# Second feed-forward of a 2-layer network: block products of sums in three of its four groups

## The chip, the cores and the metric

One core of a Trainium2 chip runs the whole program. The metric is the device time of one execution in microseconds, the median of several.

## The reference

`x` has 512 tokens of 1024 features, all in f32. The network has a first part of two layers and a second part (two attention branches, a gated feed-forward with a convolution). The change lies in the feed-forward of layer 1 of the first part, with 4096 hidden features:

```python
for i in range(DEPTH):            # DEPTH = 2
    ...                           # a mixer (mLSTM in layer 0, spatial gating in layer 1)
    h = rmsnorm(x, norm_g[i, 2]) * (1.0 + sc2) + sh2
    y = jnp.square(jax.nn.relu(h @ ffn_w1[i])) @ ffn_w2[i]
    x = x + g2 * rmsnorm(y, norm_g[i, 3])
```

`ffn_w1[i]` is 1024 x 4096 and `ffn_w2[i]` is 4096 x 1024.

## The kernel before

Each f32 matrix product is made of three TensorE products: every operand is split into a high part in fp32r and a low part, the rest, in fp32r too, and hi·hi + hi·lo + lo·hi are added up in PSUM.

Weights come in tiles of 1 MB (1024 rows x 256 columns, in SBUF 128 x 2048). SyncE loads them into two buffers, `raw0` and `raw1` (`tile_in`: it waits until the tile that was in the buffer is split). ScalarE copies a tile to its high part (`split`, L1380), VectorE subtracts that from the tile to get the low part (`rest`, L1988). The parts go in turn to the homes W (`w_both_hi`, `w_both_lo`) and U (`u_both_hi`, `u_both_lo`), each with room for two tiles.

The feed-forward works in four groups of 1024 hidden features. The up part of a group has 4 tiles with 2 blocks of 128 hidden features each: a block is 8 x 3 matmuls, weights stationary, all 512 tokens moving, into PSUM bank 0 to 3 (`tile`, L615). ScalarE makes a block's relu, square and high part (`hidden`, L1651 to L1655), VectorE its low part (`g_rest`, L2398). The down part has 2 pairs of tiles: for each of four chunks of 128 tokens 8 x 3 matmuls, hidden features stationary, two tiles of weights (512 columns) moving (`tok_pair`, L687). VectorE adds each bank to `y_acc` in SBUF (`y_part`, L1995; in group 0 it copies, L1997). Groups 1 and 2 are a loop on each engine. PSUM bank reuse, tile reuse and hidden blocks are guarded by semaphores. The first tile pair of group 0 (`first_pair`, L789) and the last pair of group 3 (`last_pair`) run together with the norms of the phases around them (`boundary`).

GpSimd has no work in a feed-forward but for single columns of powers in the boundary. Elsewhere it multiplies or adds in SBUF: a bias of the spatial gating (L2787, 128x2048 in place), gated blocks (L2791, 128x512), splits of queries and keys (L2800 to L2812). The lines L1931, L2497, L2503 are VectorE's in those phases: weight low parts, low parts of gated blocks, an addition from PSUM. L651, L660, L1003 are TensorE's at the kernel's start. The conv phase near the end is written out in full, without a loop.

## Time and profile before

| | |
|---|---|
| median of 3 runs | 2071.27 us (2071.01 to 2071.88) |
| span of the profiled execution, first to last instruction | 2068.0 us |
| time of the profiled execution itself | not given; the median lies 3.3 us above the span |
| TensorE busy | 2035.2 us, 98% |
| VectorE busy | 1153.0 us, 56% |
| ScalarE busy | 859.5 us, 42% |
| GpSimd busy | 110.2 us, 5% |
| mean granted clock of TensorE | 0.997 |
| second feed-forward (its loop's groups) | 87.04 us each |

A row of a timeline gives start and duration in us, engine, line, operation, output, inputs and shapes, the count of instructions merged in the row (x), and in brackets how long the engine stood idle before it and what ended that.
### The profile page before, as it was taken

What the parts mean: (1) busy time and instruction counts of PE and PEld (TensorE: products, weight loads), DVE (VectorE), ACT (ScalarE), POOL (GpSimd) and SP (SyncE); (2) the same over time, 40 slices, a digit from 0 to 9 for tenths busy, and PEclk for the clock granted to TensorE, in tenths of its full rate; (3) what the DMA queues carried; (4) which work ended last, traced back from release to release, by engine and by line L of the source; (5) the groups of instructions that cost most, each with busy time, mean ns of one, the idle gap of its engine ahead of it and who ended that gap; (6) DMA issues with size and microseconds to landing.
All of it is one profiled execution on the core that took longest, in us unless ns stands there. A gap on an engine that the chain in (4) does not pass through costs nothing.

```text
span 2068.0 us, 27825 instructions
## 1 busy us (share of the span) xinstructions
PE 2035.2 (98%) x10894; PEld 1699.1 (82%) x10894; DVE 1153.0 (56%) x1758; ACT 859.5 (42%) x1291; POOL 110.2 (5%) x100
## 2 busy tenths in 40 slices
PE   7999999999999999999999999999999999999998
PEld 5898888888887888988888888876777798888887
DVE  4667867566565345654233335436679746546455
ACT  3334472424246222356233246345455545324233
POOL 0000000000001025110000001000111000000000
PEclk9999999999999999999999999999999999999999
DMA  9572337576553423423332331511132132323321
GB/s 315 163 242 85 127 111 238 192 226 198 171 167 115 152 77 102 113 82 102 102 101 83 101 112 56 150 52 31 45 117 84 43 112 96 109 81 102 102 72 71
DMA packets 230377, 248.32 MB, mean 120 GB/s; under 512 B 10978, under 2 KB 223357, under 8 KB 229365
## 3 DMA queue, kind: packets, MB, share of 16 engines
q1 hardware_dynamic: 187968, 202.45, 30.8%
q10 hardware_dynamic: 42293, 44.27, 6.6%
q8 instruction: 79, 1.29, 0.3%
q14 instruction: 37, 0.30, 0.1%
HBM read 237.63 MB, written 8.42 MB: 119 GB/s over the span
## 4 chain that ended last, share of the span: by engine, by line
PE 94%; DVE 2%; ACT 1%; DMA 1%; issue 1%; DVEq 1%; SPq 0%; ACTq 0%; POOL 0%; POOLq 0%
PE bank L615 37%; PE bank L687 32%; PE bank L789 4%; PE bank L1254 4%; PE bank L718 2%; PE bank L859 2%; PE bank L1226 1%; PE bank L1003 1%; PE bank L1237 1%; PE bank L1201 1%; PE bank L1310 1%; PE bank L1295 1%; PE bank L1204 1%; PE bank L1124 1%; PE bank L754 1%; DMA ada_head<-in_ada_w 1%
## 5 line engine op out<-in xcount | busy, mean ns | idle before, releaser
L615 PE MATMUL bank<-h_hi,w_both_hi 128*128 128x512 f32 x528 | 206.6, 391 | 0.0
L615 PE MATMUL bank<-h_hi,w_both_lo 128*128 128x512 f32 x528 | 205.5, 389 | 0.0
L615 PE MATMUL bank<-h_lo,w_both_hi 128*128 128x512 f32 x528 | 205.5, 389 | 0.0
L1380 ACT ACTIVATE u_both_hi<-raw 128x2048 fp32r<-128x2048 f32 x62 | 117.1, 1906 | 174.3 <-PE bank L687 134.4
L1988 DVE TENSOR_TENSOR u_both_lo<-raw,u_both_hi 128x2048 fp32r<-128x2048 f32 x62 | 141.6, 2290 | 84.9 <-ACT u_both_hi L1380 84.9
L1988 DVE TENSOR_TENSOR w_both_lo<-raw,w_both_hi 128x2048 fp32r<-128x2048 f32 x62 | 142.0, 2290 | 74.6 <-ACT w_both_hi L1380 74.5
L615 PE MATMUL bank<-h_hi,u_both_hi 128*128 128x512 f32 x464 | 180.9, 390 | 0.0
L615 PE MATMUL bank<-h_lo,u_both_hi 128*128 128x512 f32 x464 | 180.6, 389 | 0.0
L615 PE MATMUL bank<-h_hi,u_both_lo 128*128 128x512 f32 x464 | 180.6, 389 | 0.0
L1380 ACT ACTIVATE w_both_hi<-raw 128x2048 fp32r<-128x2048 f32 x62 | 117.4, 1907 | 143.5 <-PE bank L687 91.8
L687 PE MATMUL bank<-u_both_hi,g_hi 128*128 128x512 f32 x408 | 160.1, 392 | 0.0
L687 PE MATMUL bank<-u_both_hi,g_lo 128*128 128x512 f32 x408 | 158.9, 390 | 0.0
L687 PE MATMUL bank<-u_both_lo,g_hi 128*128 128x512 f32 x408 | 158.8, 389 | 0.0
L687 PE MATMUL bank<-w_both_hi,g_hi 128*128 128x512 f32 x376 | 146.8, 390 | 0.0
L687 PE MATMUL bank<-w_both_hi,g_lo 128*128 128x512 f32 x376 | 146.3, 389 | 0.0
L687 PE MATMUL bank<-w_both_lo,g_hi 128*128 128x512 f32 x376 | 146.3, 389 | 0.0
L615 PEld LDWEIGHTS bank<-h_hi,w_both_hi 128*128 128x128 f32 x528 | 99.1, 188 | 21.7 <-issue 1.5
L615 PEld LDWEIGHTS bank<-h_hi,w_both_lo 128*128 128x128 f32 x528 | 99.1, 188 | 20.8
L615 PEld LDWEIGHTS bank<-h_lo,w_both_hi 128*128 128x128 f32 x528 | 99.1, 188 | 20.5 <-issue 0.2
L2398 DVE TENSOR_TENSOR g_lo<-tmp,g_hi 128x512 fp32r<-128x512 f32 x64 | 43.6, 689 | 108.2 <-ACT g_hi L1655 108.2
L615 PEld LDWEIGHTS bank<-h_hi,u_both_lo 128*128 128x128 f32 x464 | 87.1, 188 | 18.3
L615 PEld LDWEIGHTS bank<-h_hi,u_both_hi 128*128 128x128 f32 x464 | 87.1, 188 | 17.9
(455 smaller groups left out, 4495.9 us busy)
## 6 DMA issues: line engine op xcount, KB each, us to landing
raw<-in_ffn_w SPq DMA_DIRECT2D x64, 1024.0 KB, 5.2
ada_raw<-in_ada_w ACTq DMA_DIRECT2D x40, 1024.0 KB, 5.2
raw<-in_w_up SPq DMA_DIRECT2D x22, 1024.0 KB, 5.1
raw<-in_b_w_in SPq DMA_DIRECT2D x16, 1024.0 KB, 5.4
raw<-in_w_in SPq DMA_DIRECT2D x15, 1024.0 KB, 5.5
raw<-in_a_w_in SPq DMA_DIRECT2D x12, 1024.0 KB, 6.4
ada_head<-in_ada_w SPq DMA_DIRECT2D x8, 1024.0 KB, 12.3
raw<-in_b_w_out SPq DMA_DIRECT2D x8, 1024.0 KB, 6.3
```

The source lines that it names most:

```text
L615: mm = pe.matmul(o, x, y, start=(k == 0 and j == 0), stop=(k == kc - 1 and j == 2))
L687: mm = pe.matmul(bank[c][:].rearrange("p (s n) -> p s n", s=2), x, y, start=(k == 0 and j == 0), stop=(k == kc - 1 and j == 2))
L718: mm = pe.matmul(bank[c][:, s * 256:s * 256 + 256], x, y[:, k], start=(k == 0 and j == 0), stop=(k == KB - 1 and j == 2))
L754: mm = pe.transpose(bank[4 + p][:, at_:at_ + P], src[:, c, b * P:b * P + P], ident)
L789: mm = pe.matmul(bank[2 * s + b][:, hs], x, y, start=(k == 0 and j == 0), stop=(k == KB - 1 and j == 2))
L859: mm = pe.matmul(bank[6][:], x, y, start=(k == 0 and j == 0), stop=(k == KB - 1 and j == 2))
L1003: mm = pe.matmul(bank[m][:], x[:, k], y[:, k], start=(k == 0 and j == 0), stop=(k == KB - 1 and j == 2))
L1124: mm = pe.matmul(bank[4 + g % 4][:, c * P:c * P + P], v_all[:, c, g * P:g * P + P], w_sT[:, g, :], start=True, stop=True)
L1254: mm = pe.matmul(bank[7][:], x, y, start=(k == 0 and j == 0), stop=(k == KB - 1 and j == 2))
L1380: act.activation(slot(where, s)[0], raw[s][:], ACT.Copy).then_inc(sem("hi_done"), 1)
L1988: dve.tensor_tensor(lo, raw[s][:], f32(hi), ALU.subtract).then_inc(sem("split_done"), 1)
L2398: dve.tensor_tensor(g_lo[:, y], T[m][:], f32(g_hi[:, y]), ALU.subtract).then_inc(sem("ffn_g"), 1)
```

## The change

In groups 0, 1 and 2 of this feed-forward the down part is calculated with seven products of quarter-size blocks (Winograd's form of Strassen's scheme) in place of eight. The tokens are cut in halves, the hidden features of the group in halves, the output features in halves: with A the hidden activations (A11, A12, A21, A22) and B the weights (B11 to B22), the left factors are A11, S1, S2, S4, S3, A12, A22 in this order, where S1 = A21 - A22, S2 = S1 - A11, S4 = S2 + A12, S3 = A11 - A21; the right factors are B11, T1, T2, B22, T3, B21, T4 with T1 = B11 + B12, T2 = T1 + B22, T3 = B12 + B22, T4 = T2 + B21. Up to signs, the banks hold running sums of products and VectorE adds them to the four quarters of `y_acc`. Group 3 stays as it was, but is written out.

- TensorE: a product is 2 chunks of tokens x 4 x 3 matmuls of 512 columns, 7 of them per group. `start` is not set for products 2, 3, 4 and 6, which go on in their banks.
- GpSimd: makes T1, T2, T3 and T4 (128x2048, in place in the raw buffers) and S3 (128x1024).
- ScalarE: high parts of 11 weight tiles per group (4 up, 7 down), relu and square of the blocks (the whole f32 block is kept in `g_full`), high parts of the seven left factors.
- VectorE: low parts of the 11 weight tiles and of the left factors, S1 (in two halves), S2 and S4, and 14 additions (in group 0 partly copies).
- SyncE: 8 loads of 1 MB per group as before, into four raw buffers (`raw2` and `raw3` lie in the second halves of home U); the weights' split parts go round three slots (W0, W1, U0), the left factors' round three others.
- Semaphores with names used once are merged to make room (`x_back`, `x_again` into `x_in`; `ada_head` into `part_in`; `gates_mm`, `tok_mm`, `t5_mm` into `single_mm`); no order changes by it.

```diff
-PHASES = [... ("ffn1", 32, 2), ...
+PHASES = [... ("ffn1", 10, 2), ...
+FAST = 3
+FAST_RING = [("W", 0), ("W", 1), ("U", 0)]
+FAST_NAMES = ["u0", "u1", "u2", "u3", "B11", "B12", "B22", "B21"]
+FAST_RAW = [[0, 1, 0, 1, 2, 3, 0, 1], [0, 3, 1, 2, 0, 3, 1, 2], [1, 3, 2, 0, 1, 3, 2, 0]]
+FAST_FROM = ["B11", "B11", "B11", "B22", "B12", "B21", "B11"]
...
@@ TensorE @@
+            def fast_product(g, m):
+                which, n = fast_low(g, 4 + m)
+                pe.wait_ge(sem(which), n)
+                pe.wait_ge(sem("f_a_lo"), 8 * g + [1, 3, 4, 5, 6, 7, 8][m])
...
+                for c in range(2):
+                    if m < 2:
+                        pe.wait_ge(sem("f_g"), 8 * g + 4 + 2 * m + c + 1)
+                    else:
+                        pe.wait_ge(sem("f_added"), 14 * g + 2 * (m - 2) + c + 1)
+                    cs = slice(c * P, c * P + P)
+                    for k in range(4):
+                        for i, (x, y) in enumerate([(ah, wh), (ah, wl), (al, wh)]):
+                            mm = pe.matmul(bank[2 * (m % 2) + c][:], x[:, k, cs], y[:, k], ...)
+                    mm.then_inc(sem("f_product"), 1)
+            for g in range(FAST):
+                for j in range(0 if g else 2, 4):
+                    fast_up(g, j)
+                for m in range(7):
+                    fast_product(g, m)
@@ ScalarE @@
+            for g in range(FAST):
...
+                fast_hi(g, 4)
+                act.drain()
+                fast_a(g, 0, quarter(0, 0))
+                fast_hidden(g, 4)
+                fast_hidden(g, 5)
+                fast_hi(g, 5)
+                act.wait_ge(sem("f_s"), 4 * g + 1)
+                fast_a(g, 1, s_sum, slice(0, 2))
+                fast_hidden(g, 6)
+                fast_hidden(g, 7)
+                act.wait_ge(sem("f_s"), 4 * g + 2)
+                fast_a(g, 1, s_sum, slice(2, 4))
+                fast_hi(g, 6)
+                act.wait_ge(sem("f_s"), 4 * g + 3)
+                fast_a(g, 2, s_sum)
+                fast_hi(g, 7)
+                act.wait_ge(sem("f_s"), 4 * g + 4)
+                fast_a(g, 3, s_sum)
+                fast_hi(g, 8)
...
@@ VectorE @@
+            for g in range(FAST):
+                for i in (2, 3, 4):
+                    fast_lo(g, i)
+                fast_a_lo(g, 0, 1, quarter(0, 0))
+                fast_lo(g, 5)
+                fast_s1(g, slice(0, 2))
+                fast_a_lo(g, 1, 2, s_sum, slice(0, 2))
+                fast_s1(g, slice(2, 4))
+                fast_a_lo(g, 1, 3, s_sum, slice(2, 4))
+                dve.drain()
+                dve.tensor_tensor(s_sum[:], s_sum[:], quarter(0, 0), ALU.subtract).then_inc(sem("f_s"), 1)
+                fast_lo(g, 6)
+                fast_a_lo(g, 2, 4, s_sum)
+                for c in range(2):
+                    fast_add(g, 0, c, 0, 0, ALU.add)
+                dve.tensor_tensor(s_sum[:], s_sum[:], quarter(0, 1), ALU.add).then_inc(sem("f_s"), 1)
+                for c in range(2):
+                    fast_add(g, 1, c, 2, 1, ALU.add)
+                fast_lo(g, 7)
+                fast_a_lo(g, 3, 5, s_sum)
+                fast_lo(g, 8)
+                fast_a_lo(g, 4, 6, s3_sum)
+                for c in range(2):
+                    fast_add(g, 2, c, 0, 1, ALU.subtract)
+                fast_a_lo(g, 5, 7, quarter(0, 1))
...
+                fast_lo(g, 9)
+                fast_lo(g, 10)
+                fast_a_lo(g, 6, 8, quarter(1, 1))
...
@@ GpSimd @@
+            for g in range(FAST):
+                pool.wait_ge(sem(fast_low(g, 4)[0]), fast_low(g, 4)[1])
+                pool.wait_ge(sem(FAST_IN[g, "B12"][0]), FAST_IN[g, "B12"][1])
+                fast_sum(g, "B11", "B12")
+                pool.wait_ge(sem("f_g"), 8 * g + 4)
+                pool.wait_ge(sem("f_a_lo"), 8 * g)
+                pool.tensor_tensor(s3_sum[:], quarter(0, 0), quarter(1, 0), ALU.subtract).then_inc(sem("f_pool"), 1)
+                pool.wait_ge(sem(fast_low(g, 5)[0]), fast_low(g, 5)[1])
+                pool.wait_ge(sem(FAST_IN[g, "B22"][0]), FAST_IN[g, "B22"][1])
+                fast_sum(g, "B11", "B22")
+                fast_sum(g, "B12", "B22")
+                pool.wait_ge(sem(fast_low(g, 6)[0]), fast_low(g, 6)[1])
+                pool.wait_ge(sem(FAST_IN[g, "B21"][0]), FAST_IN[g, "B21"][1])
+                fast_sum(g, "B11", "B21")
```

`fast_hi(g, i)` makes the high part of weight tile i (0 to 3 up, 4 to 10 for products 0 to 6), once its load or sum is there and the work on the tile three before it has ended; `fast_lo` makes the low part; `fast_a` and `fast_a_lo` do the same for a left factor; `fast_s1` makes a half of S1; `fast_add` adds a bank to a quarter of `y_acc`. On SyncE, in groups 1 and 2, u0 waits for low part 7 and T3 of the group before, u1 for low part 8, u2 for low part 9 and T4, u3 for low part 10, and B11, B12, B22, B21 for low parts 0, 1, 2, 3 of their own group.

## Rows read from the trace of the kernel before

**Rows 1.** The page: busy time of each engine; the chain that ended last, by line.

```profile
PE 2035.2 (98%) x10894; PEld 1699.1 (82%) x10894; DVE 1153.0 (56%) x1758; ACT 859.5 (42%) x1291; POOL 110.2 (5%) x100
...
PE bank L615 37%; PE bank L687 32%; PE bank L789 4%; PE bank L1254 4%; PE bank L718 2%; PE bank L859 2%; PE bank L1226 1%; PE bank L1003 1%; PE bank L1237 1%; PE bank L1201 1%; PE bank L1310 1%; PE bank L1295 1%; PE bank L1204 1%; PE bank L1124 1%; PE bank L754 1%; DMA ada_head<-in_ada_w 1%
```

**Rows 2.** Chain in order of time (start us, us): loop groups, and conv.

```profile
1098.67 43.52 PE bank L615 x192
1142.19 43.52 PE bank L687 x192
...
1833.03 87.04 PE bank L615 x384
```

**Rows 3.** Busy us of PE, PEld, DVE, ACT, POOL; clock, DMA share, GB/s.

```profile
1011.63:1098.67 87.04, 87.04 (x386) 72.07 (x385) 29.11 (x24) 29.57 (x32) 0.00 (x0) 1.00 0.30 97
```

**Rows 4.** Timeline of VectorE in a group of the loop.

```profile
1153.11 0.69 DVE L1995 TENSOR_TENSOR y_acc<-y_acc,bank 128x512 f32<-128x512 f32 x1 [4.14 <-PE bank L687]
1153.72 2.29 DVE L1988 TENSOR_TENSOR u_both_lo<-raw,u_both_hi 128x2048 fp32r<-128x2048 f32 x1
```

**Rows 5.** Timeline of ScalarE in a group of the loop.

```profile
1111.51 1.90 ACT L1380 ACTIVATE u_both_hi<-raw 128x2048 fp32r<-128x2048 f32 x1
1115.03 0.60 ACT L1651 ACTIVATE tmp<-bank 128x512 f32<-128x512 f32 x1 [1.62 <-PE bank L615]
1115.71 0.63 ACT L1653 ACTIVATE tmp<-tmp 128x512 f32<-128x512 f32 x1
```

**Rows 6.** Groups by shape, 128x1024 (busy us, mean ns of one).

```profile
L2569 DVE TENSOR_TENSOR w_both_lo<-raw,w_both_hi 128x1024 fp32r<-128x1024 f32 x2 | 2.5, 1225 | 19.6 <-ACTq L1777 19.6
...
L1491 ACT ACTIVATE x_sq<-x_tok 128x1024 f32<-128x1024 f32 x4 | 4.2, 1054 | 1.9 <-DMA x_tok<-in_x 1.7
```

**Rows 7.** Groups by shape, GpSimd's addition in place.

```profile
L2787 POOL TENSOR_TENSOR v_all<-v_all,lnb_bc 128x2048 f32<-128x2048 f32 x4 | 18.5, 4614 | 38.8 <-DVE v_all L2482 38.8
```

**Rows 8.** Timelines of VectorE and GpSimd at three places.

```profile
829.90 1.18 DVE L2497 TENSOR_TENSOR h_lo<-u_T,h_hi 128x512 fp32r<-128x512 f32 x1
831.00 0.68 DVE L2503 TENSOR_TENSOR tmp<-bank,bs_bc 128x512 f32<-128x512 f32 x1
...
828.92 1.60 POOL L2791 TENSOR_TENSOR u_T<-u_T,tmp 128x512 f32<-128x512 f32 x1 [4.95 <-DVE tmp L2503]
830.48 1.75 POOL L2791 TENSOR_TENSOR u_T<-u_T,tmp 128x512 f32<-128x512 f32 x1
...
812.37 2.28 DVE L1931 TENSOR_TENSOR w_both_lo<-raw,w_both_hi 128x2048 fp32r<-128x2048 f32 x1
812.40 3.39 POOL L2791 TENSOR_TENSOR u_T<-u_T,tmp 128x512 f32<-128x512 f32 x1
...
1490.87 1.27 POOL L2802 TENSOR_TENSOR kb_swapped_lo<-kb_swapped,kb_swapped_hi 128x512 fp32r<-128x512 f32 x1
1491.05 3.23 DVE L1931 TENSOR_TENSOR w_both_lo<-raw,w_both_hi 128x2048 fp32r<-128x2048 f32 x1 [1.08 <-ACT w_both_hi L1354]
```

**Rows 9.** Timeline at a short wait of TensorE in first_pair.

```profile
933.29 0.69 DVE L2060 TENSOR_TENSOR h_lo<-h_full,h_hi 128x512 fp32r<-128x512 f32 x1 [5.06 <-ACT h_hi L1430]
934.04 0.38 PE L789 MATMUL bank<-h_hi,w_both_hi 128*128 128x256 f32 x1 [0.53 <-DVE h_lo L2060]
...
934.26 0.28 PE L789 MATMUL bank<-h_lo,w_both_hi 128*128 128x256 f32 x1
```

**Rows 10.** Window at the start (columns as rows 3); timeline of TensorE there.

```profile
27.00:30.00 3.00, 2.71 (x7) 2.16 (x8) 3.00 (x3) 0.02 (x1) 0.00 (x0) 0.50 1.10 348
...
27.29 0.76 PE L1003 MATMUL bank<-h_hi,w_both_hi 128*128 128x512 f32 x1 [3.05 <-DVE h_lo L1979]
...
31.69 0.63 PE L1003 MATMUL bank<-h_lo,w_both_hi 128*128 128x512 f32 x1
32.12 0.52 PE L1003 MATMUL bank<-h_hi,w_both_lo 128*128 128x512 f32 x1
```

**Rows 11.** DMA issues: KB each, median us to landing.

```profile
raw<-in_ffn_w SPq DMA_DIRECT2D x64, 1024.0 KB, 5.2
```

More of the change, by code:

```diff
@@ L83, with fast_raw, fast_low, fast_block @@
 HALF = S // 2
+FAST = 3
[3 more added lines that the diff above has]
+FAST_FROM = ["B11", "B11", "B11", "B22", "B12", "B21", "B11"]
+FAST_POOL = ["T1", "S3", "T2", "T3", "T4"]
+FAST_IN, loads = {}, [2] * 4
+for g, buffers in enumerate(FAST_RAW):
+    for name, r in zip(FAST_NAMES, buffers):
+        if (g, name) not in ((0, "u0"), (0, "u1")):
+            loads[r] += 1
+            FAST_IN[g, name] = (f"part_in{r}", 16 * loads[r])
+def fast_raw(g, name):
+    return FAST_RAW[g][FAST_NAMES.index(name)]
+def fast_low(g, i):
+    return "f_lo", 11 * g + i - 1
+def fast_block(g, b):
+    return 8 * g - 4 + b + 1
+def fast_pool(g, name):
+    return 5 * g + FAST_POOL.index(name) + 1
 ADA_HEAD = 8
@@ new lines, in _ @@
+            fast_split(FAST - 1, 9)
+            sp.wait_ge(sem("f_pool"), fast_pool(FAST - 1, "T4"))
+            tile_in(0, r3(0), cols(w1, FAST * 1024, 256), t0 + 2)
+            fast_split(FAST - 1, 10)
+            tile_in(1, r3(1), cols(w1, FAST * 1024 + 256, 256), t0 + 3)
+            for j in range(2, 4):
+                tile_in(j % 2, r3(j % 2), cols(w1, FAST * 1024 + j * 256, 256), t0 + 2 + j)
+            for j in range(4):
+                tile_in(j % 2, r3(j % 2), cols(w2[:, FAST, :], j * 256, 256), t0 + 6 + j)
@@ L591, in evacuated, with tile @@
                 pe.wait_ge(sem(f"evac{bk}"), q + 1)
-            def tile(t, s, q, hi, lo, kc=KB, tok=False, ready=None, after_block=None, parts=None, banks=None):
+            def tile(t, s, q, hi, lo, kc=KB, tok=False, ready=None, after_block=None, parts=None, banks=None, added=None):
                 pe.wait_ge(sem("split_done"), t + 1)
@@ L1133, in _, with fast_up @@
             last_pair("b_out", t0 + 6, q0 + 3, "U", g_hi, g_lo)
-            ffn("ffn1", "b_out", False)
+            t0, q0 = T0["ffn1"], N0["ffn1"] // 4
+            first_pair("b_out", t0, q0)
+            def fast_up(g, j):
+                which, n = fast_low(g, j)
+                pe.wait_ge(sem(which), n)
+                wh, wl = (w.rearrange("p (k n) -> p k n", k=KB) for w in fast_slot(11 * g + j))
+                for b in range(2):
+                    m, bs = 2 * (j % 2) + b, slice(b * P, b * P + P)
+                    if j < 2:
+                        pe.wait_ge(sem("f_added"), 14 * g - (1 - b if j == 0 else 3 - b))
+                    else:
+                        pe.wait_ge(sem("f_g"), 8 * g + m + 1)
+                    for k in range(KB):
+                        for i, (x, y) in enumerate([(wh, h_hi), (wh, h_lo), (wl, h_hi)]):
+                            mm = pe.matmul(bank[m][:], x[:, k, bs], y[:, k], start=(k == i == 0), stop=(k == KB - 1 and i == 2))
+                    mm.then_inc(sem("f_up"), 1)
@@ new lines, in _ @@
+            for g in range(FAST):
[3 more added lines that the diff above has]
+                    fast_product(g, m)
+            for j in range(4):
+                tile(t0 + 2 + j, j % 2, q0 + 1 + j // 2, h_hi, h_lo, parts=slot("WU"[j // 2], j % 2),
+                     added=14 * FAST - 1 if j == 0 else None)
+            tok_pair(t0 + 6, q0 + 3, "W", g_hi, g_lo, ready=(sem("ffn_g"), G0["ffn1"] + 4))
+            last_pair("ffn1", t0 + 8, q0 + 4, "U", g_hi, g_lo)
@@ new lines, in _ @@
+            for j in range(6):
+                s, q = j % 2, q0 + 1 + j // 2
+                rest(u0 + 1 + j // 2, s, "UW"[j // 2 % 2])
+                for b in range(2):
+                    if j < 4:
+                        m, y = 2 * s + b, 2 * j + b
+                        dve.wait_ge(sem("ffn_ghi"), GHI0["ffn1"] + y + 1)
+                        dve.tensor_tensor(g_lo[:, y], T[m][:], f32(g_hi[:, y]), ALU.subtract).then_inc(sem("ffn_g"), 1)
+                    else:
+                        y_part(q, 2 * s + b, 0, True)
@@ L2792, in _, with fast_sum @@
             boundary("b_out")
+            def fast_sum(g, to, more):
+                a, b = (f_raw[fast_raw(g, name)][:] for name in (to, more))
+                pool.tensor_tensor(a, a, b, ALU.add).then_inc(sem("f_pool"), 1)
+            for g in range(FAST):
+                pool.wait_ge(sem(fast_low(g, 4)[0]), fast_low(g, 4)[1])
[11 more added lines that the diff above has]
+                fast_sum(g, "B11", "B21")
             boundary("ffn1")
```

204 lines of the change are left out of this document (187 added, 17 removed).

## Prediction

> **What bounds the kernel now.** I read the page's first lines before anything else: TensorE works 98% of the span, VectorE 56%, ScalarE 42%, GpSimd 5%, and the chain that ended last is nearly all TensorE, 37% of the span at the line of the up products and 32% at that of the down products [rows 1]. Then the chain in order of time, inside the second feed-forward: 192 matmuls of 512 columns take 43.52 us, up and down alike, with no gap between them [rows 2]. That is 0.2267 us per matmul and 87.04 us per group. In such a group VectorE works 29.1 us and ScalarE 29.6, at the full granted clock [rows 3]. So a matmul taken away is worth 0.2267 us, as long as the other engines deliver in time. Their durations come next [rows 4, 5, 6, 7], then the rows where VectorE and GpSimd read SBUF together [rows 8], and last what TensorE's restart and clock do after a wait [rows 9, 10].
>
> **What is removed.** A fast group has the same 192 up matmuls, but its down part has 7 products of 24 matmuls in place of 192: 168, thus 24 fewer. The form stays (128x128 stationary, 512 columns moving), so the price stays: 24 x 0.2267 = 5.44 us a group, and 16.3 us for three. A fast group takes 81.60 us if nothing waits: products begin at 43.52, one every 5.44.
>
> **What is added, per group.** VectorE: 11 weight low parts at 2.29 [rows 4] = 25.2; the low parts of the sums of hidden blocks, six of 128x1024 and two of 128x512, 6 x 1.22 [rows 6] + 2 x 0.69 = 8.7; S1 in halves, S2 and S4: 2 x 0.69 + 2 x 1.22 = 3.8; 14 additions to y at 0.69 [rows 4] = 9.7. Together 47.4 us, where there were 29.1. The copies that group 0 has in place of additions have the same length. ScalarE: 11 weight high parts at 1.90, 8 hidden blocks at 0.60 + 0.63 [rows 5], the high parts of sums 6 x 1.05 [rows 6] + 2 x 0.63: 38.3 us. GpSimd: four weight sums of 128x2048 in place, the form of the one that takes 4.61 us in this trace [rows 7], and S3 at about 2.4: 20.8 us. Each engine has room in 81.6 us on average; the question is the second half of the group.
>
> There VectorE's order is strict. I laid it out, with time 0 at a group's first up matmul; consecutive VectorE instructions start 0.08 us before the one before has ended [rows 4], and a semaphore costs 0.04 to 0.06 us [rows 5, 9] (the block before the row at 1115.03 ends at 1098.67 + 72 x 0.2267 = 1114.99). **Without any contention:** hidden block 7 is done at 44.9 (its matmuls end at 43.52), S1's second half at 45.6, its high part on ScalarE 46.25, its low part 47.0, S2 48.2, low part 6 50.5, that of S2 51.6, two additions 52.8, S4 53.9, two additions (product 1 ends at 54.4) 55.7, low part 7 58.0, that of S4 59.1. Product 3 wants it at 59.84. So it is just in time, with 0.7 us to spare, and the gain would be all of 16.3 us.
>
> **GpSimd's sums get in the way.** The low parts and S sums read two SBUF tensors each on VectorE, as GpSimd's sums do. Where these meet in the trace, one stands until the other is over [rows 8]: the low part at 829.90 takes 1.18 us in place of 0.69, ending 0.56 after GpSimd's product has; the next GpSimd product ends 1.15 after that low part. With a longer one, GpSimd's product at 812.40 takes 3.39 in place of 1.27, ending 1.14 after a VectorE instruction of 2.28; and VectorE's weight low part at 1491.05 takes 3.23, ending 2.14 after the GpSimd instruction. They take turns: a VectorE instruction already waiting got in between two GpSimd ones that stood back to back. VectorE instructions with one PSUM operand are not held (0.68 at 831.00, beside GpSimd); the additions to y are of that kind. So a sum holds VectorE's SBUF instructions for 4.61 less 0.15 of its own start: 4.46 us.
>
> The Trainium skill (SBUF — State Buffer, section Who interferes with whom) states the same for any length: a VectorE instruction with two SBUF inputs and a GpSimd instruction that reads SBUF exclude each other for the whole instruction. By that rule the full 4.46 holds; the trace agrees for 0.6 to 2.3 us, and shows no case of 4.6.
>
> Now the same order with it. T1 runs in the up part, where VectorE has time; nothing waits. T2 may start once low part 5 is done at 38.14: S1's first half is already running, so T2 holds from 38.70 to 43.16. The first half of S1's low part, which waited, takes 43.16 to 43.72; T3 43.72 to 48.18. S1's second half has been ready since 44.9 and now ends at 48.74; ScalarE's copy 49.40, low part 50.11. **Product 1, due at 48.96, starts 1.2 us late.** S2 ends at 51.4, low part 6 at 53.6, that of S2 at 54.7, all before T4, which waits for low part 6, gets in: T4 holds 54.7 to 59.15. The additions of product 0 run beside it until 55.9, but S4 stands 3.3 us and ends at 60.2. Additions of product 1 61.4, low part 7 63.65, that of S4 64.8. Product 2 ended at 61.05: **product 3 starts another 3.8 us late.** After that there is slack again: product 4 (due 70.3) has its last input at 68.8, product 5 (75.7) at 74.1, product 6 (81.2) at 77.4, the next group (86.6) at 80.8. Each of the two restarts costs 0.06 us from semaphore to matmul and about 0.10 in the first one (0.38 where the next has 0.28) [rows 9]: 0.3 us.
>
> **Work moved that costs nothing.** Loads: eight of 1 MB per group as before, 5.2 us each [rows 11], into four buffers. The tightest is the first tile of the last group: issued after low part 9 at 74.1, it lands at 79.3, high part 81.2, low part 83.5, for a start at 86.6: 3 us of cover. The others have over 5. VectorE is then behind with two additions, which the last group covers. The wait for all 42 product halves ahead of the last group's ScalarE work ends where its U split could start before, as a buffer was only free then. Renamed semaphores add nothing. GpSimd's queue held nothing in this phase but the boundary's powers, which come after. Writing groups 1 and 2 out in place of a loop adds instructions; conv is written out and its chain has no gaps, 87.04 us for 384 matmuls [rows 2], so zero.
>
> **Sum.** -16.3 + 3 x (1.2 + 3.8 + 0.3) = -16.3 + 15.9 = -0.4 us on a span of 2068.0. The profile gives no time of its own for its execution; 3.3 us lie between its span and the median of 2071.27, and I keep these. **Forecast 2070.9 us.** Some 12 handovers a group with 0.05 us of doubt each, and 0.1 us on each of three sums, give 0.9 a group: 2068 to 2074 for this case.
>
> **Rivals.**
> *No mutual standing at this length* (GpSimd reads so slowly that both get by): then -16.3, 2055.0. For it: no row has a sum of 4.6 us beside such a VectorE instruction. Against it: [rows 8], in both directions. 0.09.
> *A long sum lets go in pieces*, say of the 1.15 us that one of 512 elements takes: S1's second half and S4 stand 1.2 in place of 3.3 us, so the stalls fall by some 4 to about 1 us a group: -13, 2058; with larger pieces anything up to the forecast. GpSimd's time grows in proportion (1.27 for 512, 4.61 for 2048), which fits one pass as well as four. 0.17.
> *The clock falls in product 3's wait.* TensorE would stand 3.8 us. At the start of the kernel it stood 3.05 us, after light work with another wait in it, and the granted clock was 0.50 from 27 to 30 us, the lower level of 1.2 GHz: matmuls of 512 columns came every 0.43 us until about 32.1 [rows 10]. Some 4.8 us at half pace lose 2.4 us; three times, +7.2: 2078. It decides for slower from two falls on. Against it: before these 3.8 us TensorE is dense, unlike there, and after the short wait before 934.04 no matmul is slow [rows 9]. 0.14, half of that with two or more falls. The Trainium skill (TensorE: Matmul & The Clock Gate, section Rules for kernel authors) advises against idle gaps of this order between bursts of matmuls; by that rule the fall comes and 2078 would hold.
> *GpSimd wins where I let VectorE go first*: T4 ahead of S2's low part makes product 2 late by 3.2 and product 3 by 1.5, 5.9 us of stall in place of 5.0: 2073.6. With T3 ahead as well, or a low part standing twice, 1.5 more a group, 2078. 0.12.
> *As forecast*: 0.48.
>
> **Numbers.** A measurement tells about 0.2%, 4.1 us. Faster by more: 0.09 + 0.15 of the pieces = 0.24. Slower by more: 0.08 of the clock, 0.05 of GpSimd's turns, 0.05 for a longer wait elsewhere in the same order = 0.18. Within: 0.58. The range for 8 in 10 runs from 2057 (all but the first rival and the smallest pieces) to 2078.
>
> **What the profile of after would show.** TensorE's group near 86.9 us instead of 81.6, with two gaps per group, at products 1 and 3, put down to VectorE's low parts of the hidden sums; low parts or S sums on VectorE of 4 to 5 us where 1.2 or 0.7 was due; GpSimd sums of 4.6 us, longer where a VectorE instruction stood first. If those VectorE instructions keep 0.69, 1.22 and 2.29 beside running sums, the first rival holds; waits of about 1 us mean pieces; a granted clock below 1.00 in products 3 and 4 means the third. I am wrong, too, if gaps stand at another product, or if loads release ScalarE's high parts.

## The result, and the profile after

The changed kernel takes 2077.23 us (median of 6, 2075.51 to 2078.69), the kernel before 2070.83 us beside it (2069.56 to 2071.88): a ratio of 1.0033, 95% interval 1.0021 to 1.0044. It is slower by 6.4 us; the forecast was 0.4 us faster. The profiled execution has a span of 2076.9 us and a time of 2078.69 us, 1.8 us more than its span.

The page, first its busy lines, which answer to [rows 1]:

```profile
PE 2027.3 (98%) x10822; PEld 1689.6 (81%) x10822; DVE 1231.7 (59%) x1797; ACT 882.9 (43%) x1300; POOL 180.5 (9%) x115
```

TensorE has 72 matmuls fewer, as it should, but is busy only 7.9 us less, not 16.3: the ones that are left have become slower somewhere. The chain in order of time shows where, in the second fast group; it answers to the two 43.52 us pieces of [rows 2]:

```profile
1014.06 43.53 PE bank L1251 x192
...
1058.95 3.87 DVE s_sum L2791
...
1070.05 4.35 DVE s_sum L2818
1074.39 1.20 DVE y_acc L2802 x2
1075.59 2.21 DVE w_both_lo L2780
1077.80 1.22 issue
1079.03 23.65 PE bank L1269 x96
1102.68 3.40 PE bank L1251 x15
```

A group lasts from 1014.06 to 1102.68, 88.62 us; before it was 87.04, predicted were 86.9. Two of VectorE's sums in SBUF are in the chain with 3.87 and 4.35 us; alone they take 0.69 and 1.22. (An instruction "stands" here when it has been issued and waits for the other engine; the timeline counts that in its duration.) Then 96 matmuls take 23.65 us. At 0.2267 us each they should take 21.76: this is a piece of pure TensorE work, with no wait in it, that is 1.89 us too long. The timelines of VectorE and GpSimd for that stretch, beside [rows 4, 8]:

```profile
1053.47 4.32 DVE L2786 TENSOR_TENSOR a_lo<-s_sum,a_hi 128x512 fp32r<-128x512 f32 x1 [0.70 <-ACT a_hi L1941]
1058.95 3.86 DVE L2791 TENSOR_TENSOR s_sum<-g_full 128x512 f32<-128x512 f32 x1 [1.16 <-ACT g_full L1934]
...
1067.63 1.22 DVE L2786 TENSOR_TENSOR a_lo<-s_sum,a_hi 128x1024 fp32r<-128x1024 f32 x1
1068.77 1.28 DVE L2802 TENSOR_TENSOR y_acc<-y_acc,bank 128x512 f32<-128x512 f32 x2
1069.96 4.43 DVE L2818 TENSOR_TENSOR s_sum<-s_sum,g_full 128x1024 f32<-128x1024 f32 x1
...
1077.72 1.21 DVE L2786 TENSOR_TENSOR a_lo<-s_sum,a_hi 128x1024 fp32r<-128x1024 f32 x1
```

```profile
1052.25 10.01 POOL L3134 TENSOR_TENSOR raw<-raw,raw 128x2048 f32<-128x2048 f32 x2 [3.00 <-DVE w_both_lo L2780]
1067.79 5.52 POOL L3134 TENSOR_TENSOR raw<-raw,raw 128x2048 f32<-128x2048 f32 x1 [5.54 <-DVE u_both_lo L2780]
```

These are T2 with T3, and T4. The first half of S1's low part ends at 1057.79, 43.73 after the group's start (predicted 43.72); S1's second half at 48.75 (48.74); S4 at 60.33 (60.2). T4 was issued 0.16 after S2's low part had begun and stood first (5.52 in place of 4.61); the two additions of product 0 ran beside it at 0.64 each. Now TensorE at the two waits, and the clock around product 3 (windows of the three us before it and the six behind, columns as in [rows 3]):

```profile
1064.30 0.47 PE L1269 MATMUL bank<-w_both_hi,a_hi 128*128 128x512 f32 x1 [1.28 <-issue]
...
1079.03 0.47 PE L1269 MATMUL bank<-w_both_hi,a_hi 128*128 128x512 f32 x1 [3.57 <-issue]
...
1080.86 0.63 PE L1269 MATMUL bank<-w_both_hi,a_hi 128*128 128x512 f32 x1
1081.29 0.63 PE L1269 MATMUL bank<-w_both_lo,a_hi 128*128 128x512 f32 x1
```

```profile
1076.00:1079.00 3.00, 0.00 (x0) 0.00 (x1) 3.00 (x3) 3.00 (x3) 0.00 (x0) 1.00 0.03 11
1079.00:1082.00 3.00, 2.97 (x9) 2.44 (x10) 3.00 (x2) 1.98 (x2) 0.00 (x0) 0.67 0.93 272
1082.00:1085.00 3.00, 3.00 (x11) 2.35 (x11) 2.91 (x5) 0.00 (x0) 0.00 (x0) 0.76 1.03 334
```

Product 1 is 1.3 us late, and product 3 starts at 64.97 of the group (predicted 64.9). The view puts both waits down to "issue", but product 3 starts 0.10 us after S4's low part has ended (1077.72 + 1.21 = 1078.93), its last input by the order above. From 1 us behind product 3's wait the matmuls come every 0.43 us, as in [rows 10], and the granted clock drops below 1.00: 1.2 GHz for a while, then 2.4 again. The same happens in all three groups: 23.64, 23.65 and 23.68 us for the 96 matmuls, after waits of 3.57, 3.57 and 3.60 us.

Where the 8.9 us between the two spans lie, by landmarks of the two chains: 0.8 before the first fast group (946.33, then 947.14), 4.8 in the three groups (239.38, then 244.19), none from there to the 192 matmuls that open the attention (151.63 and 151.65), **3.2 in the attention** (314.33, then 317.55), none after (416.33, 416.37). The attention isn't touched by the change. The 0.8 is within what traces differ by there: the same place comes at 945.38 us in short_sums and at 948.69 us in memsets, two kernels described below that differ in nothing up to it. The medians are 6.4 us apart and not 8.9; the traced execution is the slowest of its six.

### The profile page after: what moved, and what is told of

Read it like the earlier page. It is cut to its first block, busy times and chain, and to the rows that moved or that the text cites. A ratio compares the mean times of both kernels' runs of the same rounds, so it can differ in the third digit from the quotient of the medians.

```text
span 2076.9 us, 27540 instructions
## 1 busy us (share of the span) xinstructions
PE 2027.3 (98%) x10822; PEld 1689.6 (81%) x10822; DVE 1231.7 (59%) x1797; ACT 882.9 (43%) x1300; POOL 180.5 (9%) x115
## 4 chain that ended last, share of the span: by engine, by line
PE 88%; DVE 6%; ACT 2%; DMA 2%; issue 1%; DVEq 1%; ACTq 0%; SPq 0%; POOL 0%; POOLq 0%
PE bank L716 31%; PE bank L788 25%; PE bank L1251 5%; PE bank L1401 4%; PE bank L890 4%; PE bank L1269 3%; PE bank L960 2%; PE bank L1373 1%; PE bank L1104 1%; PE bank L1384 1%; PE bank L819 1%; PE bank L1348 1%; PE bank L1457 1%; PE bank L1442 1%; PE bank L1351 1%
## 5 line engine op out<-in xcount | busy, mean ns | idle before, releaser
L2240 DVE TENSOR_TENSOR w_both_lo<-raw,w_both_hi 128x2048 fp32r<-128x2048 f32 x52 | 119.1, 2290 | 69.0 <-ACT w_both_hi L1527 65.9
L716 PE MATMUL bank<-h_hi,u_both_hi 128*128 128x512 f32 x368 | 143.5, 390 | 0.0
L716 PE MATMUL bank<-h_hi,u_both_lo 128*128 128x512 f32 x368 | 143.2, 389 | 0.0
L716 PE MATMUL bank<-h_lo,u_both_hi 128*128 128x512 f32 x368 | 143.2, 389 | 0.0
L788 PE MATMUL bank<-u_both_hi,g_hi 128*128 128x512 f32 x312 | 122.7, 393 | 0.0
L788 PE MATMUL bank<-u_both_hi,g_lo 128*128 128x512 f32 x312 | 121.6, 390 | 0.0
L788 PE MATMUL bank<-u_both_lo,g_hi 128*128 128x512 f32 x312 | 121.4, 389 | 0.0
L788 PE MATMUL bank<-w_both_hi,g_hi 128*128 128x512 f32 x280 | 109.4, 391 | 0.0
L788 PE MATMUL bank<-w_both_lo,g_hi 128*128 128x512 f32 x280 | 108.9, 389 | 0.0
L2194 DVE SCALAR_TENSOR_TENSOR ada_acc<-ada_raw,c_act,ada_acc 128x256 f32<-128x256 f32 x182 | 88.2, 484 | 14.1 <-issue 0.6
L2183 DVE TENSOR_TENSOR w_both_lo<-raw,w_both_hi 128x2048 fp32r<-128x2048 f32 x29 | 67.3, 2320 | 39.9 <-ACT w_both_hi L1501 39.5
```

Source lines behind the costliest of these rows:

```text
L716: mm = pe.matmul(o, x, y, start=(k == 0 and j == 0), stop=(k == kc - 1 and j == 2))
L788: mm = pe.matmul(bank[c][:].rearrange("p (s n) -> p s n", s=2), x, y, start=(k == 0 and j == 0), stop=(k == kc - 1 and j == 2))
L2183: dve.tensor_tensor(w_lo[s][:], raw[s][:], f32(w_hi[s][:]), ALU.subtract).then_inc(sem("split_done"), 1)
L2194: i = dve.scalar_tensor_tensor(o, src[:, k], c_act[:, k:k + 1], o, ALU.mult, ALU.add)
L2240: dve.tensor_tensor(lo, raw[s][:], f32(hi), ALU.subtract).then_inc(sem("split_done"), 1)
```

## Experiments

Times are medians; ratios are to the kernel before on the same chip. "Group" is the second fast group in the chain.

**The sums' cost as a whole.** short_sums leaves out nearly all of the four weight sums, so GpSimd has next to nothing left that could hold VectorE:

```diff
-                pool.tensor_tensor(a, a, b, ALU.add).then_inc(sem("f_pool"), 1)
+                pool.tensor_tensor(a[:, 0:64], a[:, 0:64], b[:, 0:64], ALU.add).then_inc(sem("f_pool"), 1)
```

> The four weight sums on GpSimd work on 64 of 2048 columns (the rest of each sum is left out); everything else as in the changed kernel. Theory (GpSimd's sums hold VectorE's instructions with two SBUF inputs, that makes both waits per group, and the long wait lowers the clock): no wait at products 1 and 3, clock 1.00, group 81.6 us in place of 88.6, 3 x 7.0 = 21 less than the changed kernel: 2056. Rival (VectorE's own 47 us of work and the handovers bound the second half, the sums only add to it): waits of over 1 us per group stay, 2062 to 2070.

2055.91 us, ratio 0.9918 (0.9903 to 0.9934); group 81.60. The kernel gives wrong numbers, as its sums are left out. So the matmul price, the rest of the order and the loads were sized rightly, and all 16.3 us come back once the sums hold nobody.

**The clock by itself.** busy_wait fills product 3's wait with 12 matmuls that nobody reads:

```diff
+                if m == 3:
+                    for _ in range(12):
+                        pe.matmul(bank[5][:], h_hi[:, 0, 0:P], h_hi[:, 0], start=True, stop=True)
```

> Ahead of product 3 TensorE gets 12 matmuls of 512 columns into bank 5, which nobody reads: 2.7 us of the 3.6 us that it waits there. Theory (the clock falls because TensorE stands 3.6 us): the wait's end stays where it was, the clock stays at 1.00 in products 3 to 6, the group is 1.9 us shorter: 3 x 1.9 = 5.6 less than the changed kernel, 2071.6. Rival (the slow matmuls after the wait come from the weight loads that land at the same time, or from anything else than the standing): they stay slow, 2077, or more by what the extra matmuls delay.

2073.28 us, ratio 1.0006 (0.9997 to 1.0015): some 4 us below the changed kernel's median (5.6 by the two ratios), by *more* work. The chain:

```profile
1073.49 2.72 PE bank L1258 x12
1077.07 22.03 PE bank L1272 x96
1099.10 0.91 PE bank L1251 x4
```

The 96 matmuls take 22.03 in place of 23.65, and the windows behind the wait show 1.00 (22.00 to 22.04 in the three groups). The group takes 87.00: the 86.9 of the prediction. So the clock costs 1.6 us a group here, some 4.9 in all, and the wait alone what was predicted.

**Who holds whom.** memsets puts three memsets of the same buffer in place of each sum (the sums are left out), of 5.7 us together:

```diff
-                pool.tensor_tensor(a, a, b, ALU.add).then_inc(sem("f_pool"), 1)
+                pool.memset(a, 0.0)      # three times, a drain between
```

> Each of the four weight sums is replaced by three memsets of the same 128x2048 buffer (some 5.5 us of GpSimd time, longer than a sum, writing to SBUF and reading nothing from it; the sums are left out). Theory (what VectorE's two-input instructions stand for is GpSimd's reading): VectorE keeps 0.69, 1.22 and 2.29, no waits, group 81.6, 2056 as with the short sums. Rival (any GpSimd instruction on SBUF, or a late start of GpSimd's semaphores, holds them): waits at products 1 and 3 as in the changed kernel or longer, 2077 or more.

2059.43 us, ratio 0.9945 (0.9929 to 0.996); group 81.60, as in short_sums. The time is 3.5 us above that of short_sums all the same; in the two traces 3.3 us lie ahead of the first fast group (948.69 and 945.38 us). GpSimd, then VectorE:

```profile
1052.34 1.82 POOL L3134 MEMSET raw<- 128x2048 f32 x1
1054.28 1.81 POOL L3136 MEMSET raw<- 128x2048 f32 x1
1056.21 1.81 POOL L3138 MEMSET raw<- 128x2048 f32 x1
```

```profile
1054.84 0.69 DVE L2786 TENSOR_TENSOR a_lo<-s_sum,a_hi 128x512 fp32r<-128x512 f32 x1 [0.70 <-ACT a_hi L1941]
1055.62 1.22 DVE L2813 TENSOR_TENSOR s_sum<-s_sum,g_full 128x1024 f32<-128x1024 f32 x1
1056.77 2.28 DVE L2780 TENSOR_TENSOR u_both_lo<-raw,u_both_hi 128x2048 fp32r<-128x2048 f32 x1
```

VectorE keeps its 0.69, 1.22 and 2.28 us beside a GpSimd that is just as busy but only writes: what holds is GpSimd reading SBUF.

**One sum, or pieces of it.** pieces cuts each sum into four instructions:

```diff
+                for c in range(0, TILE, 512):
+                    op = pool.tensor_tensor(a[:, c:c + 512], a[:, c:c + 512], b[:, c:c + 512], ALU.add)
```

> Each weight sum is made in four instructions of 512 columns in place of one of 2048; order and work unchanged. Theory (taking turns by whole instructions): a VectorE instruction now stands at most 1.1 us in place of up to 3.9, GpSimd's sums stretch in return; product 1 waits some 0.3 in place of 1.3, product 3 some 2.6 in place of 3.8, the clock mostly stays. Group about 84.8 in place of 88.6: 2065 to 2068. Rival (GpSimd's four go through as one, or VectorE never gets in between): as the changed kernel, 2077.

2070.47 us, ratio 1.0 (0.999 to 1.0009); group 85.44, both somewhat above what was expected. VectorE:

```profile
1056.70 0.96 DVE L2791 TENSOR_TENSOR s_sum<-g_full 128x512 f32<-128x512 f32 x1 [4.48 <-ACT g_full L1934]
1058.37 1.00 DVE L2786 TENSOR_TENSOR a_lo<-s_sum,a_hi 128x512 fp32r<-128x512 f32 x1 [0.70 <-ACT a_hi L1941]
1059.46 2.15 DVE L2813 TENSOR_TENSOR s_sum<-s_sum,g_full 128x1024 f32<-128x1024 f32 x1
1061.53 3.39 DVE L2780 TENSOR_TENSOR u_both_lo<-raw,u_both_hi 128x2048 fp32r<-128x2048 f32 x1
```

No instruction stands more than about 1.1 us, but nearly each one stands: taking turns with many short pieces gives back much of what it saves. Product 3 still waits 2.76 us, and the clock stays at 1.00. It also shows that a sum in one instruction does not let go in pieces.

**The sums moved.** The next kernels change only where GpSimd's sums stand. t4_late has the last line of this diff, t3_early the others (GpSimd's blocks in that order, T3 ahead of its wait for low part 5, so that one sum fewer is left for the critical stretch), both_moves all:

```diff
-FAST_POOL = ["T1", "S3", "T2", "T3", "T4"]
+FAST_POOL = ["S3", "T1", "T3", "T2", "T4"]
-                    sp.wait_ge(sem("f_pool"), fast_pool(g - 1, "T3"))
+                    sp.wait_ge(sem("f_pool"), fast_pool(g - 1, "T2"))
...
+                pool.wait_ge(sem("f_a_lo"), 8 * g + 6)      # ahead of T4
```

> GpSimd makes T4 only after the low part of S3 (product 4's) is done; it moves the sum away from S4 on VectorE, one part of the order changed. Theory: product 1 still waits 1.3, product 3 waits some 0.8 in place of 3.6 and the clock stays at 1.00; T4 now holds product 5's low part, and product 5 waits about 1.3. Group 85.3 us in place of 88.6: 2067. Rival (the bound is VectorE's sum of work plus the sums' 4.5 us each, wherever they stand): group above 86.5, 2071 or more.

2070.3 us, 0.9991 (0.9981 to 1.0); group 85.65. That is 3.3 us above the 2067 expected, of which the longer groups explain about 1. The wait at product 3 shrinks to 0.35; product 5, which had slack, now waits 1.58.

> GpSimd's order is S3, T1, T3, T2, T4 in place of T1, S3, T2, T3, T4: T3 needs only loads and T1, so it can run in the up part where VectorE is mostly idle. Theory: product 1 does not wait; T4 comes 3 us earlier, so S4's standing ends at 56 and product 3 waits 2 us in place of 3.6, too short for the clock to fall. Group 83.7 us in place of 88.6: 2062.5. Rival (T3 is not what delays product 1): product 1's wait stays, group above 86.5, 2071 or more.

2069.75 us, 0.999 (0.998 to 0.9999); group 84.54 where 83.7 was expected: product 1 is in time, product 3 waits 2.7 to 3.5 us. The clock fell in one group of three, the third (TensorE's timeline, then the window from there):

```profile
1157.44 0.76 PE L1269 MATMUL bank<-u_both_hi,a_hi 128*128 128x512 f32 x1 [2.68 <-issue]
```

```profile
1157.00:1161.00 4.00, 3.56 (x9) 2.87 (x10) 4.00 (x4) 2.39 (x2) 0.00 (x0) 0.57 0.02 4
```

In the second group, after the same 2.68 us, it stayed at 1.00, and after 3.46 us in the first too. The expected time was 7 us too low: 2.5 of it are three groups 0.84 longer than expected, about 1.6 the fall of the clock (the 96 matmuls take 23.57 us in place of 22.02), and 2.9 is what the two traced executions lie off their medians (the changed kernel's 1.5 above, this one 1.4 below).

> Both moves of order together: GpSimd makes S3, T1, T3, T2, and T4 only after product 4's low part. Theory: product 1 does not wait; product 3's last input is ready at 59.1 us of the group, just in time for 59.84 (in group 0 some 1.2 us later than in the others, so about 0.5 late there); product 5 waits about 0.7 because T4 holds its low part. No wait is long, the clock stays at 1.00. Group about 82.4 us in place of 87.04 before: 2058 to 2060, faster than both kernels. Rival (each moved sum costs its 4.5 us somewhere else in the same half): group above 85, 2066 or more.

2063.39 us, 0.9964 (0.9951 to 0.9976), faster than both kernels, but not the 2058 to 2060 expected; group 83.24. What is left of any length is one stand that TensorE waits for, of the low part for product 5, and a wait of 1.3 to 1.6 us behind it (S1's first low part still takes 4.33, which delays nothing):

```profile
1072.45 4.75 DVE L2786 TENSOR_TENSOR a_lo<-g_full,a_hi 128x1024 fp32r<-128x1024 f32 x1
```

t4_later waits one VectorE instruction longer:

```diff
-                pool.wait_ge(sem("f_a_lo"), 8 * g + 6)
+                pool.wait_ge(sem("f_a_lo"), 8 * g + 7)
```

> The orders of both_moves, with GpSimd's last sum T4 moved once more, behind the low part of product 5 (one VectorE instruction later). In both_moves T4 held that low part for 3.5 us, and product 5 started some 1.6 us late. Theory (only what a running sum holds matters): product 5's low part takes 1.2 us again, T4 holds the next weight low part instead, product 5 waits at most 0.9 us and a group takes 82.3 to 82.8 us in place of 83.24; 1 to 3 us less than both_moves in all, about 2061, ratio 0.995. Rival: T4 now ends so late that ScalarE's high part of T4's block, the last one, makes the next group's first tile or its loads late; then the waits move to the next group's start, the group takes 83.2 us or more, and the time is that of both_moves or up to 3 us longer.

2063.38 us, 0.9963 (0.995 to 0.9976); group 83.03. A miss: the low part takes 1.21 now, but the weight low part next on VectorE takes 5.63, and product 5 needs that as well. It waits 1.13. Moving the holder by one instruction only moved the stand.

both_pieces is both_moves with the sums cut as in pieces:

> The orders of both_moves, with each of GpSimd's sums in four instructions of 512 columns. Theory (taking turns): a VectorE instruction that waits gets in after at most one piece, so T4 holds product 5's low part for at most 1.2 us in place of 3.5, and product 5 is no longer late; but every weight low part beside a sum may be held too (3.3 in place of 2.28 us), as in the run pieces. A group takes 81.8 to 82.6 us; 2062 or a little less, and no clock below 1.00 in the groups. Rival: VectorE's many short holds add up, product 3 waits again as in the run pieces (2.8 us), and a group takes 84 us or more; then about 2067, slower than both_moves.

2061.22 us, 0.9953 (0.9941 to 0.9965), the lowest median of those with all sums; group 82.85. The low part for product 5 takes 1.43, and the weight low part 3.26. The wait that is left, 1.0 us, has moved on to product 6: T4's four pieces, taking turns with VectorE, need 8.09 us in place of 4.61, and T4 is that product's factor. (Group 0 also waits 0.50 at product 3.)

**The 3.2 us in the attention.** A second trace of the kernel before (before_again) shows how much its own stretch varies:

> The kernel before once more, for a second trace of it. In the first the stretch of the second part's attention, from the 192 matmuls at 1337 us to the 192 at 1652, is 314.3 us long, in the changed kernel 317.6, though the change touches nothing there. If this is spread between executions, the second trace of before may have 316 to 318; if the change causes it, 314.3 again.

2072.21 us; the stretch takes 314.44 us there, 314.33 in the first trace. In the ten kernels so far that have the fast groups it takes 315.70 to 317.74. The chain of the changed kernel shows two pieces, then of before the ones that answer:

```profile
1501.33 6.75 DMA w_bias<-t_rows
...
1509.37 4.53 PE bank L1401 x12
```

```profile
1495.35 5.44 DMA w_bias<-t_rows
...
1502.09 2.95 PE bank L1254 x12
```

The load of the bias rows is 1.3 us longer; TensorE waits for it 2.31 us in place of 0.97; and then its first 12 matmuls are slow, by 1.58 us: the clock again. All kernels with the fast groups have the load at 6.5 to 6.9 us; the slow matmuls stand in after, short_sums, busy_wait, t4_late and t4_later, with stretches of 317.4 to 317.7, and not in the others, 315.7 to 316.0. Two candidates among the edits, each put alone into the kernel before:

```diff
-                with pe.Fori(1, 3) as g:
-                    group(g)
+                    for g in (1, 2):      # unrolled; so on the other engines
+                        group(g)
...
-                    mm.then_inc(sem("gates_mm"), 1)
+                    mm.then_inc(sem("single_mm"), 1)      # merged_sems; so the others that the change merges
```

> The kernel before, with the loop over the two middle groups of the second feed-forward written out on TensorE, VectorE, ScalarE and SyncE, and nothing else changed. It asks where the 2 us come from that the changed kernel loses outside its three groups: from the attention's first 192 matmuls to the end of its projections the trace of before has 314.3 and 314.4 us in two executions, the changed kernel 317.6, and its variants 315.9 to 317.7. Theory A (more code to fetch): the written-out loop shows 316 us or more there, and the time rises by 1 to 2 us over before. Theory B (code size does nothing; these are spreads between executions, or come from the merged semaphores): 314.3 there and a ratio of 1.000 within 0.001.

> The kernel before, with only the change's renamed semaphores: the waits that had their own semaphore share one (gates, token and table matmuls; the two later loads of x; the first loads of the modulation). Nothing of the second feed-forward is changed. Theory B2 (a shared semaphore makes a wait end later, as in-order counts need an earlier event that comes late): the attention stretch takes 316 us or more, as in the changed kernel, and the time rises by 1 to 2 us. Rival (a renamed semaphore changes nothing, as the prediction took it): 314.3 there and a ratio of 1.000 within 0.001.

unrolled 2070.96 us, 0.9998 (0.9989 to 1.0007), load 5.40, stretch 314.26; merged_sems 2071.33, 1.0 (0.9991 to 1.0009), 5.65, 314.53. Neither. Then the loads' form:

```diff
-                        tile_in(j % 2, r3(j % 2), cols(rows, j * 256, 256), t0 + 8 * g + 4 + j)
...
+                            src = cols(rows, j // 2 * 512, 512)[:, j % 2 * 4:j % 2 * 4 + 4, :]   # wide_rows
...
-                fast_in(g, "B11", rows[:, 0:4, 0:512])
+                fast_in(g, "B11", rows[:, :, 0:256])   # narrow_rows, and so B12, B22, B21
```

> The kernel before, with only the twelve down tiles of the second feed-forward's first three groups loaded in rows of 2 KB, as the changed kernel loads its blocks, into the two buffers of before (the tiles then hold other numbers than the reference's). Theory (the packets' size, or their number, shifts how the later loads lie on the DMA engines): 6144 packets fewer, the bias load at the attention's start takes 6.5 us or more in place of 5.4 to 5.7, the attention stretch 315.7 to 317.7 us in place of 314.3, and the time rises by 1.4 to 3 us, ratio 1.001. Rival (it is the four buffers and the order of the loads): 5.4 to 5.7 us, 314.3, and a ratio of 1.000.

> The changed kernel, with its twelve blocks loaded in rows of 1 KB, as before (the blocks then hold other numbers than the reference's); buffers and order stay. Theory of the packets: 187968 packets on that queue again, the bias load 5.4 to 5.7 us, the attention stretch 314.3 us, and 1.4 to 3 us less than the changed kernel: about 2075, ratio 1.002. Rival of buffers and order: the load stays at 6.5 us or more, the stretch at 315.7 to 317.7, the time at 2077. The groups keep 88.6 us either way.

wide_rows 2071.03 us, 1.0007 (0.9999 to 1.0016), load 5.50, stretch 314.36; narrow_rows 2077.68, 1.0036 (1.0023 to 1.0049), 6.58, 315.79. Not the packets either. What is left of the change's loads, the four buffers and their order, wasn't tried alone. The DMA view of the load's last three us, 1505.33 to 1508.33 after and 1499.35 to 1502.35 before (40 slices: busy tenths, GB/s), shows what the last part of the longer load looks like:

```profile
DMA  9899999999999999999875310000100001000010
GB/s 328 307 348 410 382 362 410 341 423 362 348 423 362 410 355 355 348 389 348 287 266 184 123 62 21 20 20 20 41 20 21 20 20 41 20 20 20 21 41 20
```

```profile
DMA  9999999999999999999998332000000000000000
GB/s 369 328 348 389 369 369 430 348 369 328 430 348 348 451 348 369 328 369 348 328 328 287 123 103 82 21 0 0 0 0 0 0 0 0 0 0 0 0 0 0
```

After, a tail at some 20 GB/s, the pace of one engine of 16 where all 16 give about 360, runs on for over a us. It looks as if one DMA engine were late with its share; that is read from the pace, the view names no engine. And the queue of instruction packets (16 KB each) has one packet in that load in every kernel with the fast groups, and none there in those without. So I tried to move the fetches by half a packet, in both kernels:

```diff
+            for _ in range(128):
+                pe.nop()      # pad_before, pad_after
...
+                    pe.matmul(bank[5][0:32, 0:1], cst[:, 32 * (i % 2):32 * (i % 2) + 32], cst[:, 0:1], start=True, stop=True)      # small_mm, 64 times
```

> The kernel before, with 128 empty instructions on TensorE's queue at its very start, where TensorE has nothing to do for 9.4 us. Nothing else is changed. Theory (a fetch of instructions shares a DMA engine with the load of the bias rows): TensorE's code is fetched in packets of 16 KB, some 256 instructions, so 128 more move every later fetch by half a period, 12 us: one falls 161 us into the attention stretch, inside the load of the bias rows, which takes 6.5 to 6.9 us in place of 5.4 to 5.7; the stretch takes 315.7 to 317.7 us in place of 314.3, and the kernel 1.4 to 3 us more. Rival (the fetch and the long load only coincide, the cause is in the changed kernel's own loads or buffers): fetches move, the load stays at 5.4 to 5.7 us and the stretch at 314.3. If no fetch moves, empty instructions take no room, and the run tells nothing.

> The changed kernel, with the same 128 empty instructions on TensorE's queue at its very start. Theory: the fetch that falls into the load of the bias rows moves 12 us away from it; the load takes 5.4 to 5.7 us, the stretch 314.3, the clock stays in the first products after it, and the kernel takes 1.5 to 3 us less than the changed kernel, about 2075, ratio 1.002. Rival: fetches move, the load stays at 6.5 us or more, the stretch at 315.7 or more, the time at 2077.

> The kernel before, with 64 extra matmuls of one column (32 columns of stationary data, nobody reads the result) at the very start: 24 before the first transposes, 40 before the first modulation sums, both ahead of waits. With their weight loads they are 128 TensorE instructions, half of a 16 KB packet. Theory (the fetch shares a DMA engine with the load): the fetches of the attention move by 12 us, one falls 161 us into the stretch and makes the bias load 6.5 to 6.9 us, the stretch 315.7 to 317.7 us. Rival (they only coincide): fetches move, the load stays at 5.4 to 5.7 us and the stretch at 314.3. The whole time may also move by 1 or 2 us at the kernel's start, so the load and the stretch are the measure.

> The changed kernel with the same 64 small matmuls. Theory: the fetch leaves the load of the bias rows, which takes 5.4 to 5.7 us; the stretch takes 314.3, and the kernel 1.5 to 3 us less than the changed kernel but for what the start adds. Rival: fetches move, the load stays at 6.5 us or more and the stretch at 315.7 or more.

pad_before 2070.49 us (0.9996, 0.9987 to 1.0005), pad_after 2078.06 (1.0028, 1.0017 to 1.004), small_mm_before 2071.65 (1.0001, 0.9992 to 1.001), small_mm_after 2079.42 (1.0039, 1.0026 to 1.0051); loads of 5.48, 6.68, 5.64 and 6.55 us. The fetches that matter did not move. The empty instructions added no packet. The small matmuls added one, but in small_mm_before the nearest packet starts 2.4 us ahead of the load, where before_again and pad_before have it too (2.9 us; 8.7 in the first trace of before), and small_mm_after has its own inside as before. So these four tell nothing on the cause. In all 20 traces the long load and the packet inside it go together; that it is the cause stays unproven.

## Why the prediction was wrong

**The failed step is the clock: the sum lets TensorE come back from product 3's wait at full pace, at a cost of nothing.** I had seen that it might not, and gave that a chance of 0.14, half of it with two or more falls. It fell three times of three, and in the nine such waits of narrow_rows, pad_after and small_mm_after (3.57 to 3.59 us) nine times more. In the changed kernel each fall costs 1.6 us (23.65 against 22.03 in busy_wait), less than the 2.4 that I had scaled from [rows 10]. It can cost more: in the first groups of narrow_rows and pad_after, where the first matmul behind the wait is already slow, the 96 take 24.74 and 24.57 us, 2.7 and 2.5 more than 22.03:

```profile
988.12 0.77 PE L1269 MATMUL bank<-w_both_hi,a_hi 128*128 128x512 f32 x1 [3.59 <-issue]
```

The argument against it, that TensorE is dense before the wait, was worth little: in the changed kernel it is dense, and the clock fell. By the Trainium skill (TensorE: Matmul & The Clock Gate, section Why this matters for your kernels, which the prediction gives under a wrong name) a gap of this order between bursts is to be avoided; the trace agrees, with the granted clock of 0.67 in the three us from product 3 on. t3_early shows that the length of the gap doesn't settle it: no fall after 3.46 us, one after 2.68.

The clock rival's 2078 lies close to the measured 2077.23, but in part by luck: its price per fall was too high for the falls of this trace, and the bias load, which it didn't have, makes up for most of that.

By the prediction's own steps:

- *24 matmuls fewer a group, 16.3 us*: right. short_sums gives a group of 81.60 and 2055.91 us.
- *A running sum holds VectorE's two-input SBUF instructions for its whole length; instructions with a PSUM operand aren't held; they take turns*: right, to 0.15 us at four places. The Trainium skill (SBUF — State Buffer, section Who interferes with whom) has the lock last for the whole instruction, and says that a GpSimd instruction that only writes SBUF doesn't contend; the stands of 4.3 us and the memsets without any agree with both.
- *Product 1 late by 1.2, product 3 by 3.8, restarts 0.3*: measured 1.3 and 3.6 of idle time. The two restarts are dearer than thought, some 0.3 us each: in busy_wait 48 matmuls behind product 1's wait take 11.16 us and the 96 behind product 3's 22.03, at 0.2267 each 10.88 and 21.76. Shorter waits and dearer restarts nearly cancel: the group without the clock takes 87.00 (predicted 86.9).
- *Clock, 0*: 1.6 a group, some 4.9 us.
- *Nothing outside the groups*: false. The attention takes some 1.4 us longer in each of the 13 traces with the fast groups (315.70 us or more, against 314.26 to 314.53 without), where the bias load is longer, and the clock behind it adds 1.58 in some. This was no term of the sum and no rival; its cause stays open. The two zeros that the prediction did give a reason for, written-out groups and merged semaphores, held when tried alone (unrolled, merged_sems).
- *The other rivals*: no mutual standing (0.09) and pieces (0.17) are ruled out by the VectorE rows, GpSimd winning turns (0.12) by T4, which stood behind S2's low part.

The sum with what was measured: -0.1 (three groups of 87.00 in place of 87.04) + 4.9 + 1.4 = +6.2 us, beside 6.4 between the medians. The clock behind the bias load, 0 to 1.6 us by trace, comes on top in some executions; the interval of the ratio, 4.3 to 9.1 us, leaves room for it.

## What to carry to other kernels

A change that takes 5 us of matmuls out of a stretch and puts waits of 5 us into it may not be neutral: look what the clock did after the nearest long wait and price it per wait, not as a remote case. Before GpSimd gets a long two-operand instruction, list which VectorE instructions are urgent while it runs; most of a sum's cost goes away where it starts while VectorE has slack (both_moves and both_pieces have medians 14 and 16 us below the changed kernel's by order, or order and cutting, alone). And moving the holder one instruction on helps only if the next instruction isn't due at the same product.

## What the runs showed of the hardware that was not expected

- The length of a wait alone doesn't tell whether the clock falls. It fell after 3.57 to 3.60 us (twelve of twelve, in four kernels), after 2.68 in t3_early (one of two), and not after 3.46 there (one) or 2.70 to 2.76 in pieces (none of three). At the bias load it fell after 2.14, 2.31, 2.48, 2.50 and 2.51, and not after eight waits of 2.06 to 2.31.
- It also fell where TensorE had worked without a wait of over 0.25 us for more than 30 us: ahead of the attention, behind 24 matmuls of one column (2.6 us), the next 48 matmuls take 12.59 to 12.66 us in 8 of the 20 traces and 11.06 in the other 12. Three of the eight (before_again, merged_sems, wide_rows) have no fast groups, so two executions of one kernel can differ by this 1.6 us. The first trace of before, then the second:

```profile
1324.57 11.06 PE bank L615 x48
```

```profile
1325.08 12.66 PE bank L615 x48
```

- GpSimd's memset of 128x2048 (1.82 us) doesn't hold VectorE's 128x512 to 128x2048 two-input instructions (0.69 to 2.28 us).
- A long wait can be bridged: 12 matmuls that nobody reads, 2.7 us of them, kept the clock at 1.00 in all three groups. It cost nothing that the traces show: the 96 matmuls behind take 22.03 us, and 22.02 in pieces behind an unbridged wait in which the clock stayed.
- `pe.nop()` added no fetched instruction packet (79 in before and 79 with 128 of them, in the larger of the two instruction queues).
